# A hybrid state-space and gating block on one core: a Toeplitz matrix stored in DRAM as eight shifted copies and loaded in runs of 2 KB

## The chip, the cores and the metric

The kernel runs on one core of a Trainium2 chip. The metric is the device time of one execution in microseconds (us). TensorE is called PE below, VectorE DVE, ScalarE ACT, GpSimd POOL and SyncE SP, as in the profile.

## The reference, cut to what matters

```
h    = modulate(x, g_mix, sh1, sc1);  hc = modulate(ctx, ...)
proj = h @ w_in            # S5 input u_a | gating input z_b | gate logits
y_a  = s5_mixer(u_a, u_ac) # 32 groups of 16 features, two directions, state 64 per group
y_b  = sgu_mixer(z_b)
x    = x + ga1 * ((g_a * (y_a @ w_proj_a) + g_b * (y_b @ w_proj_b)) @ w_out)
x    = x + ga2 * conv_ffn(modulate(x, g_ffn, sh2, sc2))
out  = rms_norm(x, g_final)
```

There are 256 tokens of 1024 features. The state-space mixer `s5_mixer` is a linear recurrence over the tokens. The kernel cuts the tokens into chunks of T = 8 steps. What an input does to an output in the same chunk depends only on the distance of their time steps (15 distances, `LAGS`), so for each of the 32 groups it is one 128 x 128 Toeplitz matrix: 8 input steps by 16 features on the rows, 8 output steps by 16 features on the columns. What earlier chunks do comes from a carried state.

## The kernel before, in words

The work is one program written out by hand for each engine; semaphores set the order. The stages that matter here, in PE's order from 97 to 188 us:

1. `gate_unit(0)` (L573: 32 weight tiles of one 1 MB unit of `ring_w`), the chunk inputs of the state (`chunk_inputs`, L562), the lag matrices K (L596), two more `chunk_inputs`, the gating products (L614).
2. `gate_unit(1)` to `gate_unit(5)` (L573).
3. `pe.wait_ge(s_m, 16 * T)`, then the Toeplitz products (L635, 64 of them, with `m_toep` as moving data), `gate_unit(6)`, the carried-state products (L648), which wait for the scan on DVE (`s_scan`), `gate_unit(7)`, the transposes of the result (L658), three projections (L667), the GLU product (L688), the other projections (L667) and the output product (L711).

The Toeplitz matrices are made through DRAM. K lies in PSUM as 15 lags x 16 columns for each of 128 rows (8 groups x 16 features) and 4 feature tiles. ACT copies it to `k_sb` (L897), stores it with one DMA to `k_scratch` (L899), and copies the chunk inputs of group 6 (`chunk_inputs_copied(6)`, L883). POOL waits for the store (`s_k_out`) and issues eight loads (L373), one for each input step tau. Each fills 16 partitions of `m_toep` with 32 runs of 128 floats (512 B) a partition, cut out of the 15 lags at an offset that depends on tau. `k_sb` and `m_toep` lie in the same region, so no load may start before the store has finished.

Behind the eight loads POOL waits for all of them (`s_m`), and then loads the conditioning row (`c_bc`, L377) and the 24 tiles of `mod_w` (L383; 512 KB each, nine buffers). DVE multiplies and sums these tiles (`modulation_sums`, L1421): nine of them after the scan, then the skip term of the state-space output (L1434), then seven more. The skip term is released by the transposes on PE (L658); ACT's GELU (L920) follows, and PE's GLU product (L688) waits for that.

The weights of the gate units come through a ring of four 1 MB buffers, loaded by SP (L323, L326); unit u is loaded when unit u - 4 has been multiplied. `out_w` (L330, L334) is loaded on the same queue.

Of the kernel before, what the change touches and what calls it, by code (L numbers as in the profile page):

```python
# [18 lines left out]
F32 = mybir.dt.float32  # L19
# [3 lines left out]
P = 128  # L23
# [6 lines left out]
KS = S5W // P  # L30
G, H, N = 32, 16, 64
# [3 lines left out]
T = 8  # L35
CH = TOK // T
LAGS = 2 * T - 1
# [42 lines left out]
def build(nc, x_t, x_tok, ctx_t, pk, s5raw, early_w, ring_w, out_w, up_w, ln, sgu_w, sgu_b, mod_w, c_row, g_row, out):  # L80
    with ExitStack() as ctx:
# [3 lines left out]
        def sem(name):  # L85
            return ctx.enter_context(nc.semaphore(name))

        bank = [ctx.enter_context(nc.psum_tensor(f"bank{i}", [P, 512], F32)) for i in range(8)]
# [7 lines left out]
        m_region = s5_region[:, 17408:17408 + 4096]  # L96
        scratch = m_region[:, 0:2304]
        b_raw = m_region[:, 2304:2304 + 1024].rearrange("p (r c h) -> p r c h", r=2, c=DP)
        m_toep = m_region.rearrange("p (g m) -> p g m", g=G)
        e_region = s5_region[:, 21504:21504 + 4096]  # L100
        c_raw = e_region[:, 0:1024].rearrange("p (r c h) -> p r c h", r=2, c=DP)
        b_bar = e_region[:, 1024:2048].rearrange("p (r c h) -> p r c h", r=2, c=DP)
# [10 lines left out]
        u_chunk = ctx_region[:, :].rearrange("p (g c) -> p g c", g=G)  # L113
# [85 lines left out]
        k_sb = m_region[:, 0:KS * LAGS * H]  # L199
# [10 lines left out]
        u_dram = nc.dram_tensor("u_scratch", [KS, P, T, 2 * CH], F32)  # L210
        ga1_dram = nc.dram_tensor("ga1_scratch", [1, D], F32)
        ga2_dram = nc.dram_tensor("ga2_scratch", [1, D], F32)
        k_dram = nc.dram_tensor("k_scratch", [KS, P, LAGS * H], F32)


        s_pk, s_pk2 = sem("pk_loaded"), sem("pk_rest_loaded")
# [28 lines left out]
        s_k_ps, s_k, s_k_out, s_m = sem("k_in_psum"), sem("k_evacuated"), sem("k_stored"), sem("m_loaded")  # L245
# [107 lines left out]
        def _(pool):  # L353
# [14 lines left out]
            pool.dma_start(sgu_b_sb[64:128, :, :], sgu_b[1:2].partition_broadcast(64)).then_inc(s_ln, 16)  # L368
            pool.dma_start(ln_sb, ln.partition_broadcast(P)).then_inc(s_ln, 16)
            pool.dma_start(sgu_w_sb, sgu_w).then_inc(s_ln, 16)  # L370
            pool.wait_ge(s_k_out, 16)
            for tau in range(T):
                pool.dma_start(m_toep[tau * H:(tau + 1) * H, :, :],  # L373
                               k_dram[:, :, (T - 1 - tau) * H:(2 * T - 1 - tau) * H].rearrange("m (g h) n -> h (m g) n", h=H)).then_inc(s_m, 16)
            pool.wait_ge(s_e_ps, 8)
            pool.wait_ge(s_m, 16 * T)
            pool.dma_start(c_bc, c_row.partition_broadcast(P)).then_inc(s_crow, 16)  # L377
# [23 lines left out]
        def _(pe):  # L401
# [25 lines left out]
            for k in range(KD):  # L427
                pe.wait_ge(s_sqx[k % 2], k // 2 + 1)
                mx = partial_squares(bank[6], k, TOK)
            mx.then_inc(s_part, 1)  # L430
            for k in (1, 2, 0, 3, 5, 6, 4, 7):
                by = next(e for e in range(3) if k in CTX_SQUARES[e])
                pe.wait_ge(s_sqc[by], CTX_SQUARES[by].index(k) + 1)
                mx = partial_squares(bank[7], k, 0)
# [92 lines left out]
            for half in range(2):  # L527
                u = U_V + half
                ring_ready(pe, u)
                for c in range(2):  # L530
                    for kk in range(KD // 2):
                        k = half * (KD // 2) + kk
                        mx = pe.matmul(bank[6 + c][:, :], h_x[:, k, c * P:(c + 1) * P], ring[:, u % RING, kk * 512:(kk + 1) * 512],  # L533
                                       start=(k == 0), stop=(k == KD - 1))
# [95 lines left out]
            for g2 in range(2):  # L630
                for j in range(P // H // 2):
                    for m in range(KS):
                        g = m * (P // H) + 2 * j + g2

                        mx = pe.matmul(bank[g2][m * CH:(m + 1) * CH, j * P:(j + 1) * P], u_chunk[:, g, CH:2 * CH], m_toep[:, g, :],  # L635
                                  start=(j == 0), stop=False, skip_group_check=True)
            mx.then_inc(s_toep, 1)

# [18 lines left out]
            for tau in range(T):  # L657
                mx = pe.transpose(bank[tau // 4][:, (tau % 4) * P:(tau % 4 + 1) * P], y_tok[:, tau * P:(tau + 1) * P], ident[:, :])  # L658
# [129 lines left out]
        def _(act):  # L788
# [89 lines left out]
            def chunk_inputs_copied(job):  # L878

                d, r, q0 = job // 4, (job // 2) % 2, 8 * (job % 2)  # L880
                act.wait_ge(s_e_ps, job + 1)
                col = (r * 2 + d) * PAIRS + q0
                act.activation(e_chunk[:, :, col:col + 8].rearrange("p s c -> p c s"), bank[job % E_BANKS][:, :].rearrange("p (c s) -> p c s", c=8),  # L883
                               ACT.Copy).then_inc(s_e, 1)
# [11 lines left out]
                act.wait_ge(s_k_ps, b + 1)  # L896
                act.activation(k_sb[:, 2 * b * LAGS * H:(2 * b + 2) * LAGS * H], bank[6 + b][:, 0:2 * LAGS * H], ACT.Copy).then_inc(s_k, 1)  # L897
            act.wait_ge(s_k, 2)
            act.dma_start(k_dram[:].rearrange("m p n -> p m n"), k_sb[:, :].rearrange("p (m n) -> p m n", m=KS)).then_inc(s_k_out, 16)  # L899

            chunk_inputs_copied(6)
            for j in range(1, 5):
                gate_sigmoids(j)
            act.wait_ge(s_crow, 16)
# [871 lines left out]
```

## Time and profile before

| what | value |
|---|---|
| median of 3 runs | 463.06 us (462.38 to 466.3) |
| the profiled execution's own time | 463.87 us |
| its span | 461.9 us |
| around the span | 2.0 us |
| PE busy | 450.6 us (98% of the span) |
| DVE busy | 405.8 us (88%) |
| ACT busy | 116.9 us (25%) |
| POOL busy | 45.4 us (10%) |
| moved by DMA | 98.47 MB, mean 213 GB/s |

Times are counted from the start of the span. Issuing a DMA does not count as busy. The three runs lie 3.9 us apart.

### The profile page before, as it was taken

What the parts mean: (1) busy time and instruction counts of PE and PEld (TensorE: products, weight loads), DVE (VectorE), ACT (ScalarE), POOL (GpSimd) and SP (SyncE); (2) the same over time, 40 slices, a digit from 0 to 9 for tenths busy, and PEclk for the clock granted to TensorE, in tenths of its full rate; (3) what the DMA queues carried; (4) which work ended last, traced back from release to release, by engine and by line L of the source; (5) the groups of instructions that cost most, each with busy time, mean ns of one, the idle gap of its engine ahead of it and who ended that gap; (6) DMA issues with size and microseconds to landing.
All of it is one profiled execution on the core that took longest, in us unless ns stands there. A gap on an engine that the chain in (4) does not pass through costs nothing.

```text
span 461.9 us, 7680 instructions
## 1 busy us (share of the span) xinstructions
PE 450.6 (98%) x2637; PEld 347.9 (75%) x2637; DVE 405.8 (88%) x817; ACT 116.9 (25%) x216; POOL 45.4 (10%) x73
## 2 busy tenths in 40 slices
PE   8999999999999999999999999999999999999995
PEld 5777857888888888885478888888888887444454
DVE  4599999999999948789836999999999999899974
ACT  5423355125104005201152222122122122200002
POOL 2001100002104222000000110110110111000000
PEclk9999999999999979999999999999999999999999
DMA  8994399942999999959269554564554454400002
GB/s 299 414 422 168 135 344 86 290 172 72 114 240 412 413 399 398 416 201 414 110 254 405 208 184 148 216 227 151 212 189 148 163 182 78 150 0 0 1 0 91
DMA packets 24604, 98.47 MB, mean 213 GB/s; under 512 B 7608, under 2 KB 9280, under 8 KB 16128
## 3 DMA queue, kind: packets, MB, share of 16 engines
q1 hardware_dynamic: 14592, 72.34, 44.9%
q0 software_dynamic: 5056, 18.61, 12.8%
q10 hardware_dynamic: 4928, 7.14, 4.2%
q8 instruction: 18, 0.29, 0.3%
q14 instruction: 10, 0.08, 0.1%
HBM read 95.49 MB, written 2.60 MB: 212 GB/s over the span
## 4 chain that ended last, share of the span: by engine, by line
PE 78%; DVE 15%; DMA 4%; SPq 1%; issue 1%; ACT 0%; DVEq 0%; ACTq 0%
PE bank L756 33%; PE bank L767 14%; PE bank L573 11%; DVE s_region L1052 8%; PE bank L667 6%; PE bank L711 5%; DMA s_region<-early_w 4%; PE bank L482 3%; PE bank L648 2%; PE bank L688 1%; DVE s_region L1171 1%; DVE s_region L1309 1%; PE bank L448 1%; DVE s_region L1340 1%; DVE merge_tmp L1052 1%
## 5 line engine op out<-in xcount | busy, mean ns | idle before, releaser
L756 PE MATMUL bank<-h_all,s_region 128*128 128x256 f32 x704 | 152.3, 379 | 0.2 <-ACT h_all L966 0.2
L756 PEld LDWEIGHTS bank<-h_all,s_region 128*128 128x128 f32 x704 | 133.2, 190 | 19.1 <-ACT h_all L966 0.6
L1571 DVE SCALAR_TENSOR_TENSOR ctx_region<-ctx_region,pk_sb 128x189 f32<-128x189 f32 (+2 forms) x352 | 130.1, 442 | 0.3 <-DVE ctx_region L1571 0.2
L573 PE MATMUL bank<-h_all,ring_region 128*128 128x256 f32 x256 | 58.7, 392 | 0.3 <-DVE s_region L1340 0.3
L573 PEld LDWEIGHTS bank<-h_all,ring_region 128*128 128x128 f32 x256 | 50.2, 197 | 8.3 <-issue 0.6
L767 PE MATMUL bank<-s_region,ring_region 128*128 128x512 f32 (+1 forms) x132 | 47.6, 521 | 0.0
L984 ACT ACTIVATE ctx_region<-bank 128x512 f32<-128x512 f32 x22 | 13.1, 597 | 113.3 <-PE bank L756 60.1
L767 PEld LDWEIGHTS bank<-s_region,ring_region 128*128 128x128 f32 x132 | 25.1, 190 | 22.2 <-issue 20.8
L1052 DVE TENSOR_TENSOR s_region<-s_region,power 128x2048 f32<-128x2048 f32 (+1 forms) x16 | 38.1, 2420 | 0.2
L396 POOL TENSOR_TENSOR ring_region<-gates,ctx_region 128x256 f32 x22 | 17.3, 787 | 178.1 <-ACT gates L992 178.1
L482 PE MATMUL bank<-h_all,ring_region 128*128 128x256 f32 x128 | 31.1, 388 | 0.1
L667 PE MATMUL bank<-z_region,ring_region 128*128 128x256 f32 x128 | 28.0, 379 | 0.0
L482 PEld LDWEIGHTS bank<-h_all,ring_region 128*128 128x128 f32 x128 | 23.3, 190 | 5.9 <-ACT h_all L829 2.5
L667 PEld LDWEIGHTS bank<-z_region,ring_region 128*128 128x128 f32 x128 | 24.2, 190 | 3.3
L1421 DVE SCALAR_TENSOR_TENSOR s_region<-s_region 128x1024 f32<-128x1024 f32 x20 | 23.7, 1222 | 3.3 <-DMA s_region<-mod_w 3.1
L1560 DVE TENSOR_SCALAR ctx_region<-ctx_region,pk_sb 128x256 f32<-128x256 f32 x22 | 11.5, 521 | 11.6 <-ACT ctx_region L984 10.9
L871 ACT ACTIVATE gates<-bank,pk_sb 128x256 f32<-128x256 f32 x16 | 6.7, 471 | 43.9 <-PE bank L573 43.9
L533 PE MATMUL bank<-ring_region,h_all 128*128 128x512 f32 x32 | 16.4, 594 | 0.0
L1017 ACT ACTIVATE z_region<-s_region 128x512 f32<-128x512 f32 (+1 forms) x4 | 2.3, 572 | 50.0 <-DVE s_region L1641 37.8
L829 ACT ACTIVATE h_all<-h_all,mod,scale 128x256 f32<-128x256 f32 x16 | 8.9, 594 | 22.9 <-DVE scale L1233 20.8
L521 PEld LDWEIGHTS bank<-ident,s_region 128*128 128x128 f32 x64 | 7.9, 141 | 8.8 <-issue 7.9
L711 PE MATMUL bank<-s_region,h_all 128*128 128x512 f32 (+1 forms) x40 | 14.2, 507 | 0.0
(242 smaller groups left out, 536.5 us busy)
## 6 DMA issues: line engine op xcount, KB each, us to landing
s_region<-up_w SPq DMA_DIRECT2D x33, 1024.0 KB, 5.0
ring_region<-ring_w SPq DMA_DIRECT2D x20, 1024.0 KB, 9.5
s_region<-mod_w POOLq DMA_DIRECT2D x20, 512.0 KB, 12.9
s_region<-early_w SPq DMA_DIRECT2D x4, 1024.0 KB, 21.8
s_region<-out_w SPq DMA_DIRECT2D x4, 1024.0 KB, 12.8
gates<-mod_w ACTq DMA_DIRECT2D x8, 512.0 KB, 5.4
gates<-early_w SPq DMA_DIRECT2D x2, 1024.0 KB, 10.7
s_region<-k_scratch POOLq DMA_DIRECT2D x8, 256.0 KB, 11.9
```

The lines of the kernel that those rows point to most:

```text
L396: pool.tensor_tensor(ffn_act[:, bass.ds(i * 2 + b, 1), :].rearrange("p a t -> p (a t)"), silu_sb[:, b, :], conv[:, b, TOK:2 * TOK], ALU.mu ...
L482: mx = pe.matmul(bank[m][:, cols], ring[:, U_INU + k // 4, ((k % 4) * KS + m) * P:((k % 4) * KS + m + 1) * P], h_all[:, k, cols], start=(k ...
L533: mx = pe.matmul(bank[6 + c][:, :], h_x[:, k, c * P:(c + 1) * P], ring[:, u % RING, kk * 512:(kk + 1) * 512], start=(k == 0), stop=(k == K ...
L573: mx = pe.matmul(bank[5 - j % 2][:, mm * TOK:(mm + 1) * TOK], ring[:, u % RING, (mm * KD + k) * P:(mm * KD + k + 1) * P], h_x[:, k, :], st ...
L667: mx = pe.matmul(bank[PROJ_BANK[m % 4]][:, (1 - half) * TOK:(2 - half) * TOK], ring[:, u % RING, t * P:(t + 1) * P], src[:, k, :], start=( ...
L711: mx = pe.matmul(bank[OUT_BANK[n]][:, cols], lhs(i), rhs(i)[:, cols], start=(i == 0 and n not in (3, 6, 7)), stop=(i == KD // 2 - 1), skip ...
L756: mx = pe.matmul(bank[s % 3][:, half * TOK:(half + 1) * TOK], up_ring[:, s, (half * KD + k) * P:(half * KD + k + 1) * P], h2[:, k, :], sta ...
L767: mx = pe.matmul(bank[PRODUCT_BANK[n]][:, cols], lhs(i), rhs(i)[:, cols], start=(i == 0), stop=(i == PAIRS_D - 1))
L984: act.activation(up_sb[:, j % 2, :], bank[(j % USLOTS) % 3][:, :], ACT.Copy).then_inc(s_upsb, 1)
L1052: mark(dve.tensor_tensor(o, a, b, op))
L1421: dve.scalar_tensor_tensor(out=mod_tile[t % MTS], in0=mod_tile[t % MTS], scalar=1.0, in1=c_bc4, op0=ALU.mult, op1=ALU.mult, accum_out=mod_ ...
L1571: dve.scalar_tensor_tensor(out=o, in0=a, scalar=cw[:, tile[half], (dy + 1) * 3 + dx + 1], in1=o, op0=ALU.mult, op1=ALU.add).then_inc(s_con ...
```

## The change

`k_scratch` becomes `[row p, tau, feature tile m, 128]`: eight shifted windows of 128 columns instead of the 15 lags once. ACT stores them with eight DMAs, one for each tau, each reading four pieces of 512 B a partition and writing 2 KB a partition in one piece; together 2 MB instead of 480 KB. They are issued after `chunk_inputs_copied(6)` where the one store stood before it. POOL waits for all eight (`16 * T` instead of 16) and issues its eight loads; each fills 16 partitions with eight runs of 2 KB instead of 32 of 512 B, the same 256 KB. The columns of `m_toep` are now ordered by group, then feature tile, and the matmul's index follows; its operands keep their sizes and their unit step.

```diff
-        m_toep = m_region.rearrange("p (g m) -> p g m", g=G)
+        m_toep = m_region.rearrange("p (g m n) -> p g m n", g=P // H, m=KS)
+        m_groups = m_region.rearrange("p (g n) -> p g n", g=P // H)
...
-        k_dram = nc.dram_tensor("k_scratch", [KS, P, LAGS * H], F32)
+        k_dram = nc.dram_tensor("k_scratch", [P, T, KS, P], F32)
...
-            pool.wait_ge(s_k_out, 16)
+            pool.wait_ge(s_k_out, 16 * T)
             for tau in range(T):
-                pool.dma_start(m_toep[tau * H:(tau + 1) * H, :, :],
-                               k_dram[:, :, (T - 1 - tau) * H:(2 * T - 1 - tau) * H].rearrange("m (g h) n -> h (m g) n", h=H)).then_inc(s_m, 16)
+                pool.dma_start(m_groups[tau * H:(tau + 1) * H, :, :], k_dram[:, tau, :, :].rearrange("(g h) m n -> h g (m n)", h=H)).then_inc(s_m, 16)
...
-                        mx = pe.matmul(bank[g2][m * CH:(m + 1) * CH, j * P:(j + 1) * P], u_chunk[:, g, CH:2 * CH], m_toep[:, g, :],
+                        mx = pe.matmul(bank[g2][m * CH:(m + 1) * CH, j * P:(j + 1) * P], u_chunk[:, g, CH:2 * CH], m_toep[:, 2 * j + g2, m, :],
...
             act.wait_ge(s_k, 2)
-            act.dma_start(k_dram[:].rearrange("m p n -> p m n"), k_sb[:, :].rearrange("p (m n) -> p m n", m=KS)).then_inc(s_k_out, 16)
-
             chunk_inputs_copied(6)
+            k_lags = k_sb[:, :].rearrange("p (m n) -> p m n", m=KS)
+            for tau in range(T):
+                act.dma_start(k_dram[:, tau, :, :], k_lags[:, :, (T - 1 - tau) * H:(2 * T - 1 - tau) * H]).then_inc(s_k_out, 16)
             for j in range(1, 5):
                 gate_sigmoids(j)
```

## Rows read from the trace of the kernel before

**Rows 1.** The page: busy time, and the chain that ended last by engine.

```profile
PE 450.6 (98%) x2637; PEld 347.9 (75%) x2637; DVE 405.8 (88%) x817; ACT 116.9 (25%) x216; POOL 45.4 (10%) x73
...
PE 78%; DVE 15%; DMA 4%; SPq 1%; issue 1%; ACT 0%; DVEq 0%; ACTq 0%
```

**Rows 2.** The chain in order of time, 112 to 165 us: start, length, what.

```profile
112.29 34.80 PE bank L573 x160
147.09 1.89 PE bank L635 x64
148.98 7.10 PE bank L573 x32
```

**Rows 3.** Timeline of POOL, 105 to 160 us: start, length, what, idle before.

```profile
112.52 5.01 POOL L373 DMA_DIRECT2D s_region<-k_scratch  x8 [53.94 <-DMA k_scratch<-s_region]
137.56 0.57 POOL L377 DMA_DIRECT2D s_region<-c_row  x1 [20.04 <-DMA s_region<-k_scratch]
```

**Rows 4.** Line L373, the eight loads: time from issue to landing.

```profile
DMA to landing us min/median/max: 5.7/11.9/20.1
```

**Rows 5.** Timeline of ACT, 104 to 150 us.

```profile
109.03 0.38 ACTq L899 DMA_DIRECT2D k_scratch<-s_region  x1
109.45 1.07 ACT L883 ACTIVATE s_region<-bank 128x512 f32<-128x512 f32 x1 [0.46 <-PE bank L562]
110.55 1.28 ACT L871 ACT_TABLE_LOAD   x1
119.50 0.84 ACT L871 ACTIVATE gates<-bank,pk_sb 128x256 f32<-128x256 f32 x2 [7.67 <-PE bank L573]
```

**Rows 6.** Issue times of other DMAs through DRAM (ns min/median/max).

```profile
L317 SPq DMA_DIRECT2D ctx_region<-u_scratch x8: 329/486/1497, 69.3 to 73.8; - x8
L851 ACTq DMA_DIRECT2D u_scratch<-gates x4: 326/332/360, 54.9 to 57.9; - x4
```

**Rows 7.** DMA traffic, 109.8 to 111.6 us, in 40 slices of 0.045 us; the landing of L899.

```profile
GB/s 0 0 0 149 213 299 384 384 384 320 320 341 341 320 363 384 384 320 341 405 384 363 341 384 341 341 363 363 384 341 363 427 341 214 128 64 43 21 21 21
...
q10 hardware_dynamic: 526, 0.49, 79.8%
...
k_scratch<-s_region ACTq DMA_DIRECT2D x1, 480.0 KB, 3.2
```

**Rows 8.** DMA traffic, 138 to 150 us: full-width loads of 4 and 8 KB runs.

```profile
DMA packets 1062, 4.96 MB, mean 413 GB/s; under 512 B 119, under 2 KB 119, under 8 KB 796
```

**Rows 9.** DMA traffic, 73 to 79 us: loads of 256 B runs to 16 partitions (L317).

```profile
DMA packets 2025, 0.50 MB, mean 84 GB/s; under 512 B 2025, under 2 KB 2025, under 8 KB 2025
```

**Rows 10.** DMA traffic, 114 to 126 us: the K loads; the ring load's landing.

```profile
DMA packets 430, 1.44 MB, mean 120 GB/s; under 512 B 79, under 2 KB 79, under 8 KB 429
...
q0 software_dynamic: 429, 1.43, 102.7%
...
ring_region<-ring_w SPq DMA_DIRECT2D x1, 1024.0 KB, 17.5
```

**Rows 11.** DMA queues, 112.5 to 137 us: packets, MB, share.

```profile
q0 software_dynamic: 640, 2.10, 68.5%
q1 hardware_dynamic: 212, 1.61, 28.3%
```

**Rows 12.** Timeline of SP, 119 to 121 us.

```profile
119.64 0.33 SPq L323 DMA_DIRECT2D ring_region<-ring_w  x1
```

**Rows 13.** Timeline of all engines, 150 to 210 us.

```profile
164.70 9.68 PE L573 MATMUL bank<-h_all,ring_region 128*128 128x256 f32 x32
...
168.74 1.23 DVE L1421 SCALAR_TENSOR_TENSOR h_all<-h_all,s_region 128x1024 f32<-128x1024 f32 x1 [0.23 <-DMA h_all<-mod_w]
...
174.93 2.15 DVE L1434 SCALAR_TENSOR_TENSOR ctx_region<-u_x,pk_sb,bank 128x128 f32<-128x128 f32 x8 [4.88 <-PE bank L658]
...
177.12 2.10 ACT L920 ACTIVATE u_x<-ctx_region 128x1024 f32<-128x1024 f32 x1 [0.36 <-DVE ctx_region L1434]
...
180.38 7.07 PE L688 MATMUL bank<-u_x,ring_region 128*128 128x256 f32 x32
```

**Rows 14.** Stretch 164 to 166 us: busy time of each engine, granted clock, DMA share, GB/s.

```profile
164.00:166.00 2.00, 2.00 (x16) 1.41 (x9) 0.72 (x1) 1.08 (x2) 0.00 (x0) 0.50 0.98 381
```

## The prediction

> **What bounds the kernel now.** The page's busy shares come first: PE is busy in 98% of the span, and the chain that ended last runs through PE for 78% of it [rows 1]. Then the chain around the change: from 112.3 us PE runs five gate units without a gap, 34.8 us for 160 tiles, or 6.96 us a unit. It comes to the Toeplitz products at 147.1 us and goes on at once with gate unit 6 [rows 2]. The matrix waits for PE, not PE for the matrix: POOL, which waits for the last of the eight loads, goes on at 137.6 us [rows 3], and the last load, issued near 116.9 us (the end of POOL's 5.0 us of issues less one), landed 20.1 us later, at 137.0 us [rows 3, 4]. So the matrix is there 10.1 us before it is wanted. A faster load can't be seen in the time; a slower one can, from 10.1 us on. I also read the DMA traffic, because it runs nearly full from the first K load on: 120 GB/s at a busy share over 100% while K loads [rows 10], 413 GB/s afterwards [rows 8].
>
> **ACT's part.** One store of 0.38 us [rows 5] goes, eight come. A store to DRAM from ACT took 0.33 us to issue, and a series of eight 128 KB transfers of 512 runs each, as here, took up to 1.5 us for one and at most 6.0 us in all (first start 69.3, last start 73.8) [rows 6]. They stand behind the copy of group 6, which PE releases at 109.45 us in any case [rows 5], so moving it up wins nothing. Behind them are a table load of 1.28 us and the sigmoids that PE releases at 119.5 us, with 7.67 us of idle time before them [rows 5]. From 110 us, 2.6 to 6 us of issues and 1.3 us of table load end by 117.3 us. Cost: nothing; cover left: 2.2 us.
>
> **The stores.** Bytes go from 480 KB to 2.10 MB, in 4096 pieces of 512 B instead of 512 of 960 B. The old one shows traffic in 31 slices of 0.045 us, 1.4 us, so 351 GB/s, or 16 x 1.4 / 512 = 44 ns of one DMA engine per 960 B piece [rows 7]. Runs of 8 KB at the full-width 413 GB/s would take 8192 / 25.8 = 317 ns [rows 8]. A line through both gives 7.5 ns + 0.038 ns a byte, 27 ns for 512 B, and 4096 x 27 / 16 = 6.9 us. Lower bound: the bytes at 351 GB/s, 6.0 us. Upper bound: what a 256 B piece cost in the u loads, 6 us x 16 / 2025 = 47 ns [rows 9], gives 12.1 us. I take 6.9, because the 960 B store is the same direction and path. The old store had 0.9 us ahead of its traffic and 0.9 us behind it (109.03 to 109.94, 111.35 to 112.2) [rows 5, 7]. With a first issue at 110.0 (109.5 to 110.5) all stores have landed at 110.0 + 0.9 + 6.9 + 0.9 = 118.7 us, against 112.2 before (bounds 117.3 to 124.4). POOL follows 0.3 us later, as it did (112.2 to 112.52) [rows 3].
>
> **The loads.** This is the disputed price. Runs become four times longer, but each load still fills only 16 partitions. Rate now: 120 GB/s [rows 10], 16 x 12 / 2793 = 69 ns per 512 B piece. The other loads to 16 partitions ran at 84 GB/s with 256 B [rows 9], while full-width loads get 413 [rows 8]. Three readings. (a) The narrow target limits: the rate stays, 2.10 MB / 0.120 = 17.5 us of traffic. (b) The run's length limits, on the line through 256 B and 512 B (47 and 69 ns, so 0.083 ns a byte): 196 ns for 2 KB, 12.6 us. (c) The loads run as full-width ones: 5.1 us, about POOL's 5.0 us of issues. A 960 B piece cost 44 ns when it moved between DRAM and all 128 partitions, less than the 69 ns of a 512 B piece here; so it is not the length of the run that makes the piece dear, and I take (a), with (c) as the lower end. Then the time from POOL's first issue to the last landing stays as it was, 137.0 - 112.5 = 24.5 us, which holds 1.61 MB of ring loads too [rows 11]. The matrix is ready at 119.0 + 24.5 = 143.5 us. One more ring load comes within reach (they are issued every 6.96 us), 1.05 MB at 413 GB/s, 2.5 us: 146.0 us. Wanted at 147.1. No stall, by 1.1 to 3.6 us.
>
> The Trainium skill bears on this. "SBUF — State Buffer", section "Door 1: The DMA port swizzle", says that DMA bandwidth depends on how many of the 16 SBUF ports the partitions reach, and its map gives 16 neighbouring partitions 4 ports; a quarter of its 435 GB/s is 109 GB/s, whatever the run. The trace's 120 GB/s is near it, a little above. By that figure the eight loads would take 19.3 us of traffic, 1.8 us more than by the row.
>
> **The ring.** The load of gate unit 5 is issued at 119.64 us and needed 17.5 us to land behind the K loads, at 137.1 [rows 10, 12]; PE wants it at 112.3 + 4 x 6.96 = 140.1. After the change the K loads are issued at the same moment, not 7 us before it, so it has less ahead of it. No cost.
>
> **What waits behind the matrix.** POOL loads the conditioning row and the `mod_w` tiles only after all eight loads. They start at 144.0 to 146.5 instead of 137.6 us. DVE already waited for the ninth tile at 168.74 us, finished it at 169.97, and then stood 4.88 us for PE's transposes [rows 13]. The traffic after the matrix is work at a full rate: c row, nine tiles, two `out_w` units and two ring units are 9.4 MB, 23 us at 0.41 MB/us, from 148.5 to about 171.5; the other bound is the whole shift, 168.7 + 7 = 175.7. So DVE ends the nine between 172.8 and 177.0 instead of 170.0, and the skip term starts 0 to 2.1 us late. PE asks for the GELU at 180.4 and has it at 179.2 [rows 13]: 1.2 us of cover. Cost 0 to 0.9 us; I put 0.5 into the sum.
>
> **The rest.** PE's 64 Toeplitz products (1.89 us [rows 2]) keep shape and step: 0. Sum against the profiled execution: 463.87 + 0.5 = 464.4 us. That execution lies 0.8 us above the median, so the forecast is 463.06 + 0.5 = 463.6 us.
>
> **Rivals.**
>
> 1. *The long runs are fast* ((b) or (c)): the matrix is ready between 125 and 141 us. PE has no gap there to close, so the time stays at 463.1. For it: the piece price did rise less than its bytes from 256 to 512 B. Against: the comparison with the 960 B piece. The Trainium skill sides with it: "Perfetto Trace Analysis", section "DMA Optimizations", names transfers under 2 KB as costly and advises larger ones; the trace's 84 and 120 GB/s fit that as well as they fit a narrow target.
> 2. *The stores and the late loads put PE in a wait* (the other side). Stores of 12.1 us, landed at 124.4, then 0.3 + 24.5 + 2.5 make the matrix ready at 151.7 us: PE stands 4.6 us before L635. It decides from 147.1 us on, that is from stores some 1.1 us slower than I take if the extra ring load is served first, 3.6 us if not. Such a gap can also cost clock: between 164 and 166 us PE had a granted 0.50, the 1.2 GHz level of its two (1.2 and 2.4 GHz), after the carried-state products, and its gate unit took 9.68 us instead of 6.96 [rows 13, 14], 2.7 us. The late tiles add up to 0.9. Price: 463.1 + 4.6 to 8.2 = 467.7 to 471.3 us. Against: it needs the upper bound of the store price, which comes from a load.
> 3. *A lower-clock stretch moves.* If the one at 164 us goes, 460.4 us, without the change doing it by its own traffic; small.
> 4. *It doesn't do what it says*: nothing gets faster because the loads keep their rate. That is my own forecast's case.
>
> **How the numbers follow.** Forecast (loads at the old rate, stores near 7 us, 0 to 3 us of PE wait): 0.48. Rival 1: 0.33. Rival 2: 0.16. Rival 3: 0.03. One per cent, 4.6 us, is about what a measurement of this kernel can tell from no change, since three runs of the same kernel lay 3.9 us apart. Faster by over 1%: 0.02; slower: rival 2 and the tail of the forecast, 0.17; within: 0.81. The range takes in the spread of the runs below (461.2) and most of rival 2 above (469.0).
>
> **What would show it.** In the profile after: eight ACT stores from about 110 us, ended by 116; the last landed near 118.7 (12 us of traffic would mean the upper bound); POOL's first K load near 119.0; traffic at some 120 GB/s during the K loads (a rate of 160 or more would mean rival 1); POOL's c row at 144 to 146.5; no PE gap ahead of L635; DVE's idle time ahead of the skip term shrunk from 4.88 us to below 2. The prediction is wrong if PE waits for the K loads for more than a few us, if the ring loads come late behind the stores, or if the granted clock falls in another place than before.

## The result, and the profile after

The changed kernel takes 467.43 us (median of 5 runs, 465.95 to 468.0), the kernel before, timed beside it, 462.38 us (5 runs, 460.74 to 466.3): ratio 1.0099, with a 95% interval of 1.0063 to 1.0135 (the two medians alone give 1.0109). It is slower, by an amount that stands right at the one per cent that I called the limit of a measurement. The profiled execution took 467.43 us, its span 465.6; before, 463.87 and 461.9. So the two profiles show 3.7 us of the difference, and it is their difference that is traced below.

The page of the changed kernel: busy shares, the chain that ended last by engine, and the bytes moved. These lines answer to [rows 1].

```profile
PE 449.4 (97%) x2637; PEld 346.7 (74%) x2637; DVE 406.6 (87%) x817; ACT 116.4 (25%) x216; POOL 44.6 (10%) x73
...
PE 75%; DMA 18%; POOL 2%; DVE 1%; ACTq 1%; issue 1%; SPq 1%; ACT 1%; DVEq 0%; POOLq 0%
...
HBM read 95.49 MB, written 4.20 MB: 214 GB/s over the span
```

PE's busy time hardly changed. What changed is who leads to the end: the DMA's part of the chain went from 4% to 18%. The chain itself names them (start, length, what):

```profile
114.54 4.74 DMA k_scratch<-s_region
...
123.27 25.31 DMA s_region<-k_scratch
...
152.85 20.14 DMA s_region<-mod_w
...
174.55 15.38 DMA s_region<-mod_w
...
191.18 1.35 DVE z_region L1443 x4
...
192.58 7.61 PE bank L667 x34
```

Before, the chain ran from PE to PE through this stretch [rows 2]. Now it goes stores, K loads, `mod_w` tiles, DVE's gated output, and only then PE. The timelines of POOL and ACT answer to [rows 3] and [rows 5]:

```profile
119.57 4.23 POOL L374 DMA_DIRECT2D s_region<-k_scratch  x8 [60.87 <-DMA k_scratch<-s_region]
149.15 0.57 POOL L377 DMA_DIRECT2D s_region<-c_row  x1 [25.36 <-DMA s_region<-k_scratch]
```

```profile
109.68 5.92 ACTq L902 DMA_DIRECT2D k_scratch<-s_region  x8
115.63 1.28 ACT L871 ACT_TABLE_LOAD   x1 [4.88 <-issue]
119.78 0.84 ACT L871 ACTIVATE gates<-bank,pk_sb 128x256 f32<-128x256 f32 x2 [2.87 <-PE bank L573]
```

POOL starts 7.1 us later and goes on 11.6 us later. ACT's 5.9 us of issues cost nothing: it still stands idle for 2.87 us before the sigmoids. PE, in the places of [rows 2] and [rows 13]:

```profile
148.71 1.95 PE L635 MATMUL bank<-s_region,ctx_region 128*32 128x128 f32 x64 [1.33 <-DMA s_region<-k_scratch]
...
165.74 7.17 PE L573 MATMUL bank<-h_all,ring_region 128*128 128x256 f32 x32
...
181.63 8.61 PE L688 MATMUL bank<-u_x,ring_region 128*128 128x256 f32 x32 [2.55 <-ACT u_x L921]
...
192.58 20.99 PE L667 MATMUL bank<-z_region,ring_region 128*128 128x256 f32 x96 [0.62 <-DVE z_region L1443]
```

Three waits that the kernel before didn't have: for the matrix 1.33 us, for the GELU 2.55, for the gated output (`z_region`) 0.62. The sum along PE: the Toeplitz products start 1.6 us later; gate unit 7 takes 7.17 instead of 9.68 us, since the stretch at half clock [rows 14] is gone, and the carried-state products before it take 0.8 us less (with a gap between them 0.2 us longer), so PE is 1.3 us *ahead* of the kernel before when it asks for the GELU (179.08 against 180.38 us). It waits 2.55, then the GLU product takes 8.61 instead of 7.07 us. The windows (us from and to, length; busy time of PE, its weight loads, DVE, ACT, POOL with instructions; granted clock, DMA share, GB/s) show why: the granted clock was 0.68 from 182 to 186 us (1.00 in the kernel before), and 1.00 from 164 to 166 us, where it had been 0.50:

```profile
182.00:186.00 4.00, 4.00 (x14) 3.28 (x14) 1.46 (x4) 1.28 (x1) 0.55 (x1) 0.68 1.01 412
...
164.00:166.00 2.00, 2.00 (x66) 1.80 (x58) 1.23 (x2) 0.15 (x1) 0.00 (x0) 1.00 0.99 404
```

-1.3 + 2.55 + 1.54 + 0.62 = 3.4 us, of the span's 3.7. DVE's timeline says where the GELU's delay is from:

```profile
161.02 1.23 DVE L1422 SCALAR_TENSOR_TENSOR s_region<-s_region 128x1024 f32<-128x1024 f32 x1 [5.51 <-DMA s_region<-mod_w]
...
176.00 1.23 DVE L1422 SCALAR_TENSOR_TENSOR h_all<-h_all,s_region 128x1024 f32<-128x1024 f32 x1 [0.24 <-DMA h_all<-mod_w]
177.23 2.15 DVE L1435 SCALAR_TENSOR_TENSOR ctx_region<-u_x,pk_sb,bank 128x128 f32<-128x128 f32 x8
...
184.80 1.23 DVE L1422 SCALAR_TENSOR_TENSOR s_region<-s_region 128x1024 f32<-128x1024 f32 x1 [2.54 <-DMA s_region<-mod_w]
```

The ninth tile is summed at 177.2 us instead of 170.0. The 4.88 us in which DVE stood idle ahead of the skip term [rows 13] are used up, the skip term starts 2.3 us late, and the tiles after it are waited for too. The DMA traffic is of the same size. From 138 to 200 us the engines are full in both kernels, and they move this much, before and after:

```profile
DMA packets 5322, 25.17 MB, mean 406 GB/s; under 512 B 602, under 2 KB 610, under 8 KB 3901
```

```profile
DMA packets 4949, 23.55 MB, mean 380 GB/s; under 512 B 563, under 2 KB 571, under 8 KB 3588
```

1.62 MB less, which is 4.0 us at 406 GB/s. The changed kernel moved some 200 GB/s from 138 to 146 us, while K loads and ring loads were under way together, and the kernel before some 400 from 136 us on. So the full-rate stream of tiles and weights starts later, by about the time that the kernel lost. That the one makes the other is for the experiments to show.

### The profile page after: what moved, and what is told of

The parts are those of the page before. It is cut to its first block, busy times and chain, and to the rows that moved or that the text cites. A ratio compares the mean times of both kernels' runs of the same rounds, so it can differ in the third digit from the quotient of the medians.

```text
span 465.6 us, 7688 instructions
## 1 busy us (share of the span) xinstructions
PE 449.4 (97%) x2637; PEld 346.7 (74%) x2637; DVE 406.6 (87%) x817; ACT 116.4 (25%) x216; POOL 44.6 (10%) x73
## 4 chain that ended last, share of the span: by engine, by line
PE 75%; DMA 18%; POOL 2%; DVE 1%; ACTq 1%; issue 1%; SPq 1%; ACT 1%; DVEq 0%; POOLq 0%
PE bank L756 33%; PE bank L767 14%; DMA s_region<-mod_w 8%; DMA s_region<-k_scratch 5%; PE bank L482 5%; PE bank L711 5%; PE bank L667 5%; DMA s_region<-early_w 4%; PE bank L548 3%; PE bank L533 3%; PE bank L521 2%; PE bank L562 2%; PE bank L573 1%; PE bank L448 1%; DMA k_scratch<-s_region 1%; ACTq L902 1%
## 5 line engine op out<-in xcount | busy, mean ns | idle before, releaser
L573 PE MATMUL bank<-h_all,ring_region 128*128 128x256 f32 x256 | 56.2, 380 | 0.3 <-DVE s_region L1341 0.3
L573 PEld LDWEIGHTS bank<-h_all,ring_region 128*128 128x128 f32 x256 | 48.4, 190 | 7.4 <-DVE s_region L1341 0.6
L482 PE MATMUL bank<-h_all,ring_region 128*128 128x256 f32 x128 | 31.1, 388 | 0.0
L667 PE MATMUL bank<-z_region,ring_region 128*128 128x256 f32 x128 | 28.2, 380 | 0.6 <-DVE z_region L1443 0.6
L482 PEld LDWEIGHTS bank<-h_all,ring_region 128*128 128x128 f32 x128 | 23.3, 190 | 5.7 <-ACT h_all L829 2.3
L667 PEld LDWEIGHTS bank<-z_region,ring_region 128*128 128x128 f32 x128 | 24.2, 190 | 4.2 <-DVE z_region L1443 1.0
L1561 DVE TENSOR_SCALAR ctx_region<-ctx_region,pk_sb 128x256 f32<-128x256 f32 x22 | 11.9, 542 | 11.6 <-ACT ctx_region L985 10.9
L548 PE MATMUL bank<-h_all,ring_region 128*128 128x256 f32 x64 | 14.0, 379 | 0.0
```

What stands on the lines that cost most here:

```text
L482: mx = pe.matmul(bank[m][:, cols], ring[:, U_INU + k // 4, ((k % 4) * KS + m) * P:((k % 4) * KS + m + 1) * P], h_all[:, k, cols], start=(k ...
L548: mx = pe.matmul(bank[2 + i][:, mm * TOK:(mm + 1) * TOK], ring[:, u % RING, (mm * KD + k) * P:(mm * KD + k + 1) * P], h_x[:, k, :], start= ...
L573: mx = pe.matmul(bank[5 - j % 2][:, mm * TOK:(mm + 1) * TOK], ring[:, u % RING, (mm * KD + k) * P:(mm * KD + k + 1) * P], h_x[:, k, :], st ...
L667: mx = pe.matmul(bank[PROJ_BANK[m % 4]][:, (1 - half) * TOK:(2 - half) * TOK], ring[:, u % RING, t * P:(t + 1) * P], src[:, k, :], start=( ...
```

## The experiments

Theory A: the long runs load no faster, the stores only push the loads 7 us back, and what follows them is late. Theory B: the long runs do help. Theory C: the delay matters little, the extra traffic or ACT's issues do. Each kernel below was timed beside the kernel before on the same chip, with 6 or 12 runs, against 22 to 35 of the kernel before. The runs of one kernel differ in their mean granted clock and with it in time (more on this at the half tiles), so some comparisons below are also made among runs with 0.996 or more, called "at a like clock".

**Short runs, in the changed kernel.** Eight stores as in the change, but the copies lie tile by tile, so the loads have runs of 512 B again.

```diff
-k_dram = [P, T, KS, P]      loads: "(g h) m n -> h g (m n)"
+k_dram = [T, KS, P, P]      loads: k_dram[tau] "m (g h) n -> h (m g) n"
```

> The changed kernel, but each of the eight copies is stored tile by tile and loaded in runs of 512 B, as in the kernel before; the stores' source pieces (512 B), the number of stores, their place and every wait stay. Theory A (the loads are limited by their 16 target partitions, whatever the run): the K loads keep their 120 to 123 GB/s, the matrix is ready within 1 us of the changed kernel's (148.6 us), time 467.4 +- 1.5 us. Rival B (the run's length does buy something, the changed kernel merely lost more elsewhere): the loads take 1.4 times as long or more (from 17 us of traffic to 24), PE waits 5 us or more before the Toeplitz products, time above 471 us.

469.72 us, ratio 1.0135 [1.0094, 1.0177]. Between the two theories: the K loads' rate falls from 121 to 101 GB/s (windows below), yet POOL goes on at 149.17 us, as in the changed kernel (149.15). What the long runs save goes to the ring: from 119.5 to 148.6 us its queue moved 3.38 MB in the changed kernel and 2.83 here. The tiles meet more traffic afterwards, and PE waits 3.88 us for the GELU instead of 2.55. The time is above theory A's 465.9 to 468.9 us and below the 471 of theory B. The long runs are worth something, but not what four times the length would give if the run were the limit. The intervals of 1.0135 and 1.0099 overlap, so in the time the benefit isn't shown; it is in the rate.

**Late loads, in the kernel before.** No extra store; POOL waits until gate unit 1 has been multiplied, so the old loads start 0.7 us after those of the change do.

```diff
             pool.wait_ge(s_k_out, 16)
+            pool.wait_ge(s_unit, U_GATE + 2)
```

> The kernel before, with its one store of 480 KB and its loads of 512 B runs, but POOL also waits until gate unit 1 has been multiplied (119.4 us) before it issues the K loads; the changed kernel issued its first at 119.57 us, the kernel before at 112.5. Nothing is added but the delay. Theory A (the loss is only that the loads start 7 us later, by the longer stores): matrix ready at 146 to 149 us, DVE's tiles late, GELU wait on PE, time 466 to 468.5 us. Rival C (the 1.6 MB of extra stores, their 4096 pieces, or ACT's 5.9 us of issues cost the time by themselves): time 462 to 464 us.

470.52 us, 1.0153 [1.0111, 1.0195]. POOL's loads run from 120.30 us and it goes on at 150.75. PE, for the matrix and for the gated output:

```profile
150.31 1.96 PE L636 MATMUL bank<-s_region,ctx_region 128*32 128x128 f32 x64 [3.01 <-DMA s_region<-k_scratch]
...
194.24 20.99 PE L668 MATMUL bank<-z_region,ring_region 128*128 128x256 f32 x96 [2.12 <-DVE z_region L1443]
```

Between them it waits 2.39 us for the GELU. The delay alone gives a loss of this size, 2 us more than the 468.5 that theory A allowed, and seemingly more than the change's (the intervals meet at 1.011 to 1.0135). Theory C isn't needed for the loss. From 128 to 136 us, where nearly nothing but K loads moves, the rate is 121 GB/s with runs of 2 KB and 101 in both kernels with 512 B. That pair is the widest: in the kernel before, whose loads start 7 us sooner, the same stretch of the loads (120 to 128 us) shows 112 GB/s, and with half the tiles (below) the same stretches show 104 with 512 B and 123 with 2 KB. So the long runs give back between 8% and 22% of the rate. The windows 128 to 136 us of the changed kernel, of the short runs and of the late loads:

```profile
128.00:136.00 8.00, 8.00 (x39) 7.04 (x38) 7.53 (x27) 0.84 (x2) 0.00 (x0) 1.00 1.02 121
```

```profile
128.00:136.00 8.00, 8.00 (x39) 7.04 (x38) 7.52 (x27) 0.84 (x2) 0.00 (x0) 1.00 1.05 101
```

```profile
128.00:136.00 8.00, 8.00 (x39) 7.06 (x38) 7.52 (x27) 0.84 (x2) 0.00 (x0) 1.00 1.05 101
```

**Two queues, in the changed kernel.** ACT issues four of the eight loads after its stores. In one kernel POOL has tau 0, 2, 4, 6 and ACT 1, 3, 5, 7; in the other POOL has 0, 1, 4, 5 and ACT 2, 3, 6, 7, so that the two queues' targets lie 32 partitions apart.

```diff
-            for tau in range(T):
+            for tau in (0, 2, 4, 6):            # other kernel: (0, 1, 4, 5)
...
+            act.wait_ge(s_k_out, 16 * T)
+            for tau in (1, 3, 5, 7):            # other kernel: (2, 3, 6, 7)
+                act.dma_start(m_groups[tau * H:(tau + 1) * H, :, :], ...).then_inc(s_m2, 16)
```

> The changed kernel with the K loads split over two queues: POOL loads input steps 0, 2, 4, 6, ACT (behind its stores) 1, 3, 5, 7, so that the two loads in flight aim at partitions 0-15 and 16-31, then 32-47 and 48-63, and so on. Theory A in its narrow form (a load is limited by what its 16 partitions can take, and partition ranges 0-15 and 16-31 have separate ways in): the K traffic doubles to about 220 to 240 GB/s, the matrix is ready near 131 to 137 us, and the time falls to 462 to 464 us. Rival D (each piece is dear for the engine that moves it, whatever the target): 120 GB/s together, matrix near 148 us, time 467 +- 1.5 us.

> As the two-queue kernel, but POOL loads input steps 0, 1, 4, 5 and ACT 2, 3, 6, 7, so that the two loads in flight aim at partitions 0-15 and 32-47, then 16-31 and 48-63, 64-79 and 96-111, and so on. If partitions 32 apart share a way in (the port map of the Trainium skill's page SBUF - State Buffer, section Door 1: The DMA port swizzle, says so), the K traffic stays at 110 to 130 GB/s in spite of two queues and the time at 466 to 468.5 us. If a second queue alone is what helps, it is as fast as the other two-queue kernel: over 200 GB/s and 462 to 464 us.

Neighbouring targets: 463.84 us, 0.9998 [0.9969, 1.0026]. Targets 32 apart: 466.69 us, 1.0074 [1.0042, 1.0105]. The first wins most of the loss back. Not all of it: 11 of its 12 runs had a granted clock of 0.996 or more, at a median of 463.65 us, and the 12 such runs of the kernel before stand at 461.52, so at a like clock some 2 us stay. That the second wins anything isn't shown, since its interval and the change's (from 1.0063) overlap. Same bytes, same runs, same queues; only the pairing of the partitions differs. The window 128 to 136 us of the first and of the second:

```profile
128.00:136.00 8.00, 8.00 (x39) 7.06 (x38) 7.52 (x28) 0.84 (x2) 0.00 (x0) 1.00 1.04 168
```

```profile
128.00:136.00 8.00, 8.00 (x39) 7.06 (x38) 7.49 (x28) 0.84 (x2) 0.00 (x0) 1.00 1.06 125
```

The first window has 0.16 MB of a ring load in its last 2 us; from 128 to 134 us, with next to nothing but K loads, the rates are 165 and 131 GB/s. So which partitions are filled at the same time bears on the rate of 120 GB/s, which is what the forecast took. But a second set of partitions gave 1.4 times the rate and not the 220 to 240 GB/s expected, and POOL went on at 142.67 us and not at 131 to 137, so the target isn't the only limit. The Trainium skill, "SBUF — State Buffer", section "Door 1: The DMA port swizzle", has partitions 32 apart on the same port and 16 apart on others: the two rates agree with the map.

**The extra stores, in the kernel before.** Eight stores of the same shape as the change's into an unused buffer, from a region that no load overwrites; POOL's wait is as before (its loads start 0.7 us later, at 113.24 us).

```diff
+            for tau in range(T):
+                act.dma_start(spare_dram[:, tau, :, :], spare[:, :, (T - 1 - tau) * H:(2 * T - 1 - tau) * H]).then_inc(s_spare, 16)
             for j in range(1, 5):
```

> The kernel before with eight more stores added behind the copy of group 6, of the same sizes and in the same place as those of the change, from a region that is not touched to a DRAM tensor that nobody reads; K keeps its own store, and POOL's loads wait only for that one. It has all of the change's extra traffic and all of ACT's issues (5.9 us), and the loads are still issued at 112.5 us. Theory A: the stores' 7 us of traffic lie beside the first K loads; the matrix is ready up to 7 us later than 137.0 (near 141 to 145), still ahead of PE's 147, tiles 4 to 7 us late, time 462.5 to 465 us. Rival C (ACT's issues or the stores' pieces cost by themselves): 466 us or more.

467.98 us, 1.0088 [1.0053, 1.0123]: missed, and in the range of the rival, theory C. 2 MB of stores cost about what the whole change does, though no load waits for them. (ACT waits for them, in a line that the cut above leaves out, before it works on the conditioning row; that held it 0.3 us.) They share the engines with the K loads, which are through at 143.06 us instead of 137.56. ACT's issues took 15.57 us, one of them 9.0 alone, where the changed kernel's took 5.92:

```profile
109.86 15.57 ACTq L906 DMA_DIRECT2D spare_scratch<-s_region  x8
```

PE waits 2.0 us for the gated output, 1.2 for ACT's gate sigmoids and 0.6 for the GELU. The wait for the sigmoids is ACT's part, and the changed kernel doesn't have it. How much of this run's time is the traffic and how much are the issues isn't parted. Theory A needs wider words all the same: what pushes the `mod_w` stream back costs, be it a late start or more traffic ahead.

**Free tiles, in the changed kernel.** POOL doesn't wait for the K loads before it issues the conditioning row and the tiles.

```diff
-            pool.wait_ge(s_m, 16 * T)
```

> The changed kernel without POOL's wait for the matrix ahead of the conditioning row and the mod_w tiles (their place in memory is free once the chunk inputs are done), so that nine tiles are queued behind the K loads at 124 us instead of 149.7. It parts the two ways in which late K loads can cost time. If the late tiles are the larger part (theory A as the trace after shows it: a GELU wait of 2.6 us, a y_a wait of 0.6 us and the low clock behind them, against 1.3 us for the matrix): the GELU and y_a waits go, DVE stands for PE's transposes again, the wait for the matrix stays or grows by the tiles' share of the traffic (1 to 4 us), time 463.5 to 466.5 us. If the matrix wait is what counts: no faster than 467.

466.48 us, 1.0066 [1.0041, 1.009]. The time is at the upper edge of the range, but the waits were foreseen the wrong way round: the wait for the matrix went, those for the GELU (2.3 us) and the gated output (2.1) stayed. POOL issued the row 26 us earlier, and ACT had it only 7 us sooner (149.84 against 157.19 us), 1.2 us after the last K load had landed in the changed kernel:

```profile
123.24 0.57 POOL L376 DMA_DIRECT2D s_region<-c_row  x1
```

```profile
149.84 1.06 ACT L905 ACTIVATE s_region<-s_region 128x1024 f32<-128x1024 f32 x1 [7.60 <-DMA s_region<-c_row]
```

The row and the tiles are held up mostly by the traffic ahead of them, not by POOL's wait. That undoing the wait wins anything isn't shown: its interval and the change's overlap.

**Tiles first, in the changed kernel.** The row and four tiles go ahead of the K loads.

```diff
+            pool.wait_ge(s_e_ps, 8)
+            pool.dma_start(c_bc, ...)
+            for t in range(4): pool.dma_start(mod_tile[t], ...)
             pool.wait_ge(s_k_out, 16 * T)
```

> The changed kernel with the conditioning row and the first four mod_w tiles loaded ahead of the K loads (issued at about 110 us). The matrix gets later, the tiles earlier. Stores and 2.6 MB of tiles share the DMA engines until about 125 us, the matrix is ready near 152 to 155 us, and PE waits 4 to 7 us there. If the two ways of losing time add up as I read them, the GELU and y_a waits go and the matrix wait takes their place: 466 to 470 us. If the tiles alone set the time: under 464.

472.22 us, 1.0173 [1.0126, 1.022]: worse than expected. The GELU and the gated output are on time now and nobody waits for them. But the stores share the engines with the tiles, POOL's first K load goes out at 129.87 us, the matrix comes 6.3 us late, and the Toeplitz products after that wait take 3.64 us instead of 1.9, at a granted clock of 0.50:

```profile
153.76 3.64 PE L637 MATMUL bank<-s_region,ctx_region 128*32 128x128 f32 x64 [6.26 <-DMA s_region<-k_scratch]
```

The wait is in the range foreseen (4 to 7 us). The rest of the miss is clock: 1.7 us in these products, and later 1.6 in the carried-state products and 1.7 in gate unit 7 (8.87 us), where the granted clock was 0.86 from 164 to 174 us and 0.77 from 174 to 183. In that later place the kernel before lost as much without such a wait [rows 13, 14], so only the first 1.7 us stand right behind the gap of 6.3.

**Two queues, in the kernel before.** The same split for the old loads, without the extra stores.

```diff
-            for tau in range(T):
+            for tau in (0, 2, 4, 6):
...
+            act.wait_ge(s_k_out, 16)
+            for tau in (1, 3, 5, 7):
```

> The kernel before (one store of 480 KB, runs of 512 B) with the K loads split over POOL's and ACT's queues, so that neighbouring ranges of 16 partitions are filled at the same time. The K traffic rises from 113 to about 150 GB/s and the matrix is ready near 130 to 133 us instead of 137. PE has no wait there to lose, so theory A: time as before, 461 to 463.5 us, ratio 0.995 to 1.003. A rival in which an earlier matrix and earlier tiles are worth something would show a ratio below 0.995.

463.12 us, 0.9999 [0.9971, 1.0026], as expected no gain; but POOL went on at 139.32 us and not at 130 to 133. At a like clock this kernel is even 0.8 us behind (11 runs, median 463.07 us, against 18 with 462.23), and PE waits 0.78 us for the gated output. The loads of 512 B runs on two queues were not through sooner than on one. Their rate from 120 to 128 us was 130 GB/s, where one queue gave 112 (the kernel before, then this one) and two queues with runs of 2 KB give 165 in their stretch. So beside the partitions the length of the run counts, and by these numbers more with two queues than with one. Ring loads ran beside their tail; no run parts that from the rest.

```profile
120.00:128.00 8.00, 8.00 (x39) 7.04 (x38) 7.79 (x13) 1.18 (x3) 0.00 (x0) 1.00 1.04 112
```

```profile
120.00:128.00 8.00, 8.00 (x39) 7.04 (x38) 7.79 (x13) 1.36 (x4) 0.00 (x0) 1.00 1.16 130
```

**Half the tiles, in both kernels.** Only two of the four quarters (1 KB of each partition's row) of each `mod_w` tile are loaded, so half of the modulation weights are missing from the result and half of the stream's bytes are gone.

```diff
-                pool.dma_start(mod_tile[t % MTS], mod_w[t]...)
+                pool.dma_start(mod_tile[t % MTS][:, 0:2, :], mod_w[t]...[:, 0:2, :])
```

> The changed kernel, with only the first half of every mod_w tile of this stage loaded (256 KB instead of 512 KB; the sums read stale data in the other half, so the modulation vectors are wrong). All waits, DVE's 24 sums and the K path stay. Theory E (what sets the time in both kernels is when DVE has the tiles and so the gated output y_a at 187 to 194 us; a late K only pushes the tile stream back): the GELU wait of 2.6 us and the y_a wait go, the matrix wait of about 1.3 us stays, and the time falls from 467.4 to 461 to 464 us. Rival F (the loss is the matrix wait and low clock on PE, the tiles are only a companion): at least 466 us.

> The kernel before with the same halves of the mod_w tiles left out (wrong modulation vectors). Theory E: this kernel too stands at the edge of its tile stream, so it falls by 1 to 3 us, to 460 to 462 us, and the distance between before and after shrinks from 4.5 to about 1.3 to 2 us, the matrix wait. If the kernel before is bound by PE alone, as I read its one profile: unchanged at 462.4 to 463.1.

Changed kernel 461.54 us, 0.9981 [0.9945, 1.0018]; kernel before 461.0 us, 0.9956 [0.9922, 0.9991]. Both ran on the same chip: the distance between the medians is 0.5 us, where the whole tiles gave 5.0. The K loads of the one are still 7.6 us later than those of the other (POOL goes on at 147.06 against 139.47), but PE waits neither for the matrix nor for the GELU nor for the gated output in either. The wait for the matrix, 1.33 us in the changed kernel, is not gone by the halving: these loads were through 2.1 us sooner than in the changed kernel's profile, before any tile was asked for. So part of the 1.33 us is spread between executions. The two other waits are gone with the tiles' bytes. That is the plainest run for theory A: the late matrix costs through the tiles behind it. DVE in the kernel before, with half the tiles, has more idle time ahead of the skip term than with whole ones [rows 13]:

```profile
171.86 2.16 DVE L1434 SCALAR_TENSOR_TENSOR ctx_region<-u_x,pk_sb,bank 128x128 f32<-128x128 f32 x8 [6.09 <-PE bank L658]
```

The kernel before gained 0.4% by it. Does the clock alone make that? Its 35 executions on this chip fall into groups by the mean granted clock of the whole span: 23 with 0.996 or more took 460.9 to 463.4 us (median 462.2), 10 with 0.992 or less took 464.2 to 467.2 (median 466.0), and 2 lay between. With half the tiles, nine executions had 0.996 or more, at a median of 460.9. So at a like clock 1.3 us are gained: the tiles were at the edge before the change too.

**`out_w` later, in the kernel before.** SP loads two 1 MB units of `out_w` as soon as the Toeplitz products are done, into the stretch in which the tiles come. Here they follow the last projection unit. A second kernel adds the two queues.

```diff
-                    sp.wait_ge(s_toep, 1)
-                    for i in (2, 3):
-                        sp.dma_start(w_out_units[:, i, :], out_w[i]).then_inc(s_wo[i], 16)
...
+            for i in (2, 3):                     # after the loop over the units
+                sp.dma_start(w_out_units[:, i, :], out_w[i]).then_inc(s_wo[i], 16)
```

> The kernel before with nothing left out; the two out_w units that SP loads at 149 us, in the middle of the tile stream, are loaded behind the last projection unit at about 188 us (they are wanted at 208 us). That takes 2.1 MB, 5 us of traffic, out of the tiles' way. Theory E: tiles earlier, y_a as early as PE allows, time 459 to 461.5 us, ratio 0.993 to 0.998, faster than both kernels. If PE alone binds: 462.4 to 463.1. If the units come too late for the output product: above 464.

> The same, and the K loads split over POOL's and ACT's queues as in the two-queue kernel on the base of before. Theory E: the two reliefs of the tile stream overlap, since PE is the bound once y_a is on time: 458.5 to 461.5 us, within 1 us of the version with late out_w alone.

461.43 us, 0.9973 [0.994, 1.0006], and with two queues 461.35 us, 0.9957 [0.9923, 0.9991]. These are the fastest versions found here that compute the whole reference. The second is 0.4% under the kernel before (the interval ends 0.1% under it), where the changed kernel is 1.0% over it. The two queues add nothing that shows: at a like clock the medians are 461.12 and 461.22 us, 1.1 and 1.0 us under the kernel before. In the first, DVE has the idle time ahead of the skip term back, and PE goes through from the GLU product to the projections in one piece (DVE's and PE's timelines):

```profile
171.79 2.15 DVE L1432 SCALAR_TENSOR_TENSOR ctx_region<-u_x,pk_sb,bank 128x128 f32<-128x128 f32 x8 [5.32 <-PE bank L656]
```

```profile
184.14 22.61 PE L665 MATMUL bank<-z_region,ring_region 128*128 128x256 f32 x104
```

**What ties them together.** The projections' second part (L667) can't start before DVE has the gated output, and DVE has it when the sixteenth tile is summed. From that start to the end of the span:

| kernel | PE starts the second part | span | rest |
|---|---|---|---|
| changed | 192.58 | 465.6 | 273.0 |
| short runs | 193.98 | 467.0 | 273.0 |
| late loads | 194.24 | 467.4 | 273.2 |
| extra stores | 190.33 | 464.5 | 274.2 |
| two queues, 32 apart | 190.89 | 465.6 | 274.7 |
| free tiles | 190.60 | 465.8 | 275.2 |
| two queues | 187.84 | 462.5 | 274.7 |
| before, two queues | 186.61 | 460.4 | 273.8 |

In all eight PE waited for the gated output there, and the rest is 273.0 to 275.2 us. So the span moves with the arrival of the tiles, to within 2.2 us.

## Why the prediction came out as it did

The forecast was 463.6 us with a range of 461.2 to 469.0; it was 467.43. The range held it, in its slower half, and the likeliest case was 3.8 us too low. That the range held is luck in good part: its upper end was taken from rival 2, whose condition, slow stores, did not come. The forecast's own terms, 463.1 us and at most 0.9, reach to 464.0. And 1.0099 stays within the one per cent, to which 0.81 was given, by a hair. One of the signs named beforehand for a wrong prediction did come: the granted clock fell in another place than before.

- *What bounds the kernel.* Right for PE. That a faster load can't show fits the run with two queues in the kernel before, though its K loads were not through sooner, so it was not put to a hard test. But I took the 10.1 us of cover ahead of the matrix as the cover of the whole chain. The tiles behind the matrix had none to speak of: with half of their bytes the kernel before gains 1.3 us at a like clock. My rows hid it. In that profile gate unit 7 lost 2.7 us to the clock [rows 13, 14], and PE never met the tiles; in the changed kernel PE was 1.3 us ahead and did.
- *ACT's part.* 5.9 us of issues (said 2.6 to 6), hidden. Right.
- *The stores.* The windows show 6.9 us of traffic at some 300 GB/s (said 6.9) and a thin tail of some 1.5 us behind it (said 0.9), the last landed at about 119.3 us (said 118.7), POOL's first load at 119.57 (said 119.0). Right, 0.6 us short. I priced them only by what waits for them; the run with the extra stores shows that 2 MB of traffic ahead of or beside the loads costs by itself, 0.9% there (with ACT's blocked issues in it).
- *The loads.* Reading (a) had the rate right, 121 GB/s, but not the whole cause. The pair with two queues shows that the target's partitions matter; the short runs show that the run's length is worth 8% to 22% of rate beside it, which (a) didn't have. The 120 GB/s of [rows 10] held the start of the loads too (158 GB/s from 114 to 116 us); from 120 to 128 us the kernel before ran at 112. Two errors, the start counted in and the length left out, cancelled. "It is not the length of the run that makes the piece dear" goes too far.
- *When the matrix is ready.* Said 143.5 to 146.0, measured 148.6, and PE waited 1.33 us where I had no wait. This term was short by 2.6 us: 0.6 from the stores, and most of the rest from the ring. I allowed 1.61 + 1.05 = 2.66 MB of ring traffic before the last K load; the queues show 3.38 MB between 119.5 and 148.6 us, and the 0.72 MB more are 1.7 us at 413 GB/s:

```profile
q0 software_dynamic: 640, 2.10, 52.4%
q1 hardware_dynamic: 460, 3.38, 44.9%
```

- *The ring.* Right, no cost to the gate units. A load issued together with the K loads went first (landed in 9.3 us instead of 17.5), and that is what the K loads then paid.
- *What waits behind the matrix.* This is the step that failed. The mechanism stood there, the size was wrong: 0.5 us, at most 0.9. (The working counts the full-rate traffic from 148.5 us, a time that no row and no sum before it gives.) Measured: the ninth tile summed at 177.2 us (said 172.8 to 177.0), the GELU waited for 2.55, a lower clock after that wait 1.54, the gated output 0.62 us. I followed the tiles to the first stage that needs them, the skip term, and not to the second, the seven further tiles and the gated output, though the engines were full up to 200 us. And the 1.2 us of cover at the GELU were counted from a PE that had just lost 2.7 us to the clock. Whether the GELU wait brought the lower clock isn't shown: after waits of 3.0 us (late loads, for the matrix) and 3.1 us (two queues 32 apart, for the GELU) the granted clock was 1.00.
- *Rival 1* is out: the rate with K loads alone was 119 to 123 GB/s, not 160 or more. *Rival 2* had the sign and nearly the price (467.7 to 471.3), but for another reason: the stores kept to the middle price, and PE's stall is mostly behind the tiles. *Rival 3*, the lower clock moves, came true in both directions at once: 3.3 us back at 160 to 173 us, 1.54 lost at 182.

Two things stay open. What puts the low-clock stretch at 164 us in some executions and not in others wasn't found; of the kernels built on the one before, the profiles of the two queues, the extra stores, the late loads and the later `out_w` have a granted clock of 1.00 from 150 to 192 us. And the 5.0 us between the medians are more than the 3.7 of the profiles; the profiled execution before lies 1.5 us over its median with that stretch in it, which has the right sign and size.

## What to carry to other kernels

A transfer that lands well before its user isn't free to move while others queue behind it: follow the stream of full-rate traffic that starts after it, to each stage that waits for a part of it, and compare the bytes that the full stretch moves in both versions. Before a layout is changed to lengthen runs, look at how many partitions a load fills: here four times the run gave 8% to 22% of rate, and two queues that filled neighbouring sets of 16 partitions at once gave 40%. And before cover is taken from a profile, ask whether a stretch at a lower clock lent it.

## What the runs showed of the hardware

- Loads to 16 partitions on one queue ran at 101 to 112 GB/s in runs of 512 B and 121 to 123 in runs of 2 KB, less than a third of the 413 GB/s of full-width loads [rows 8], with the engines' busy share at 1.0 all the while. From 120 to 128 us of the kernel before, such loads moved 0.90 MB and the ring load issued at 119.64 us [rows 12] nothing.
- Two queues of such loads, runs of 2 KB: 165 GB/s with targets 16 partitions apart, 131 with targets 32 apart (128 to 134 us). With runs of 512 B and targets 16 apart: 130.
- The landing of a full-width ring load next to narrow loads went with its place in time: issued 0.35 us after the first of them it landed in 9.3 us, issued 7 us after it in 17.5 [rows 10, 12], on a queue of its own in both cases.
- Eight stores of 256 KB took ACT 5.9 us to issue on their own, and 15.57 us when the K loads of POOL ran beside them (14.63 beside the row and four tiles). ACT does nothing else in that time.
- Right behind a wait of 6.3 us PE had a granted clock of 0.50, its 1.2 GHz level, and 64 Toeplitz products took 1.7 us longer. After waits of 3.0 and 3.1 us in two other kernels the granted clock stayed at 1.00.
- The kernel before has two groups of executions by mean granted clock, with medians 3.8 us apart (above), so one profile of it tells the time of a stage no better than that.
